# A hybrid layer on one core: the first dense weights in two transfers, h of tile 0 made by two engines, and finer waits for the first dense product

## The reference

```python
mod = silu(c) @ w_ada + b_ada            # six rows of 1024: sh1, sc1, gt1, sh2, sc2, gt2
h   = rms_norm(x, g_norm1) * (1 + sc1) + sh1
z   = h @ w_in + b_in                    # 1024 x 5376: u | v | q | k | v | gate A | gate B
ya  = gmlp_spatial(gelu(u), gelu(v))     # layer norm of v, 128 x 128 mixing by head
yb  = attention(rope(q), rope(k), v)     # windows of two chunks of 64, sinks
x   = x + gt1 * ((sigmoid(gA) * (ya @ w_o_a) + sigmoid(gB) * (yb @ w_o_b)) @ w_out)
h2  = rms_norm(x, g_norm2) * (1 + sc2) + sh2
x   = x + gt2 * moe(h2)                  # top 4 of 32 experts, 1024 x 2048 and 1024 x 1024 each
out = rms_norm(x, g_final)
```

## Time and profile before

| | us |
|---|---|
| median of 3 runs | 1270.43 (1270.15 to 1270.64) |
| the profiled execution | 1271.66 |
| its span, first to last instruction | 1269.9 |
| TensorE busy | 1041.1 (82%) |
| VectorE busy | 435.4 (34%) |
| ScalarE busy | 203.6 (16%) |
| mean granted TensorE clock | 0.913 |

### The profile page before, as it was taken

One profiled execution on the slowest core, in us unless ns is written; L12 is line 12 of the kernel. 1 busy time (PEld: TensorE's weight loads), 2 busy tenths in 40 slices (PEclk: granted clock), 3 DMA queues, 4 the chain that ended last, 5 costly groups with the idle time before them and its releaser, 6 DMA issues.

```text
span 1269.9 us, 26048 instructions
## 1 busy us (share of the span) xinstructions
PE 1041.1 (82%) x10163; PEld 507.8 (40%) x10164; DVE 435.4 (34%) x1050; ACT 203.6 (16%) x381; POOL 12.2 (1%) x39
## 2 busy tenths in 40 slices
PE   4799999977999678665999999999765679957774
PEld 1667777763444123221444444444222224422231
DVE  1885878875322113111222232233111113211122
ACT  2221223032121001000111112111100002100011
POOL 1100000000000000000000000000000000000000
PEclk9899999986999879877999999999878789987888
DMA  9987876697999999999969999939999997999996
GB/s 345 371 283 244 288 250 238 227 387 291 427 426 425 425 426 424 426 425 423 426 288 424 427 426 424 424 122 427 427 426 423 426 426 291 427 426 425 425 426 256
DMA packets 73035, 474.39 MB, mean 374 GB/s; under 512 B 7512, under 2 KB 9496, under 8 KB 39036
## 3 DMA queue, kind: packets, MB, share of 16 engines
q1 hardware_dynamic: 69888, 469.39, 90.2%
q10 hardware_dynamic: 2588, 3.03, 0.8%
q0 software_dynamic: 480, 0.83, 0.3%
HBM read 472.17 MB, written 1.06 MB: 373 GB/s over the span
## 4 chain that ended last, share of the span: by engine, by line
PE 50%; SPq 24%; DMA 19%; issue 3%; DVE 3%; ACT 1%; DVEq 0%; ACTq 0%
PE bank L1731 16%; DMA gate_up<-in_w_down_dram 14%; SPq L403 13%; PE acc L1364 13%; PE bank L1766 8%; SPq L391 8%; DMA down<-in_w_down_dram 3%; PE acc L1693 2%; PE bank L1675 2%; DMA gate_up<-in_w_in_dram 1%; DMA gate_up<-in_w_ada_dram 1%; PE bank L1681 1%; SPq L380 1%; SPq L515 1%; PE bank L1751 1%
## 5 line engine op out<-in xcount | busy, mean ns | idle before, releaser
L1731 PE MATMUL bank<-gate_up,mod 128*32 128x512 f32 x2512 | 337.4, 668 | 114.9 <-DMA gate_up<-in_w_gate_up_dram 94.9
L1731 PEld LDWEIGHTS bank<-gate_up,mod 128*32 128x32 f32 x2512 | 82.7, 117 | 305.6 <-issue 174.5
L1766 PE MATMUL bank<-gate_up,mod 128*32 128x256 f32 x2528 | 148.6, 381 | 11.3 <-DMA gate_up<-in_w_down_dram 9.9
L1364 PE MATMUL acc<-gate_up_r 128*128 128x512 f32 (+1 forms) x544 | 135.2, 395 | 7.5 <-DVE down_r L840 7.5
L787 ACT ACTIVATE front<-front 128x256 f32<-128x256 f32 x50 | 20.8, 416 | 727.2 <-DVE front L1298 727.2
L1298 DVE TENSOR_SCALAR front<-bank 128x256 f32<-128x256 f32 x50 | 21.2, 425 | 336.2 <-PE bank L1731 336.2
L1364 PEld LDWEIGHTS acc<-gate_up_r 128*128 128x128 f32 x544 | 100.6, 192 | 33.7 <-DVE down_r L840 8.0
L1766 PEld LDWEIGHTS bank<-gate_up,mod 128*32 128x32 f32 x2528 | 76.6, 110 | 70.7 <-DMA gate_up<-in_w_down_dram 17.3
L1314 DVE TENSOR_TENSOR mod<-bank,mod 128x256 f32<-128x256 f32 x50 | 21.2, 425 | 219.2 <-PE bank L1766 219.2
L1731 PE MATMUL bank<-down,mod 128*32 128x512 f32 x448 | 63.3, 690 | 27.0 <-DMA down<-in_w_gate_up_dram 24.8
L1218 DVE TENSOR_SCALAR front<-front 128x2 f32 x100 | 22.9, 229 | 154.1 <-issue 152.7
(11 more groups left out here) (309 smaller groups left out, 764.1 us busy)
## 6 DMA issues: line engine op xcount, KB each, us to landing
gate_up<-in_w_gate_up_dram SPq DMA_DIRECT2D x87, 2048.0 KB, 37.1
gate_up<-in_w_down_dram SPq DMA_DIRECT2D x96, 1024.0 KB, 34.5
down<-in_w_gate_up_dram SPq DMA_DIRECT2D x21, 2048.0 KB, 35.0
gate_up<-in_w_ada_dram SPq DMA_DIRECT2D x12, 2048.0 KB, 13.9
x_room<-in_w_gate_up_dram SPq DMA_DIRECT2D x12, 2048.0 KB, 34.1
down<-in_w_down_dram SPq DMA_DIRECT2D x22, 1024.0 KB, 35.4
gate_up<-in_w_in_dram SPq DMA_DIRECT2D x10, 2048.0 KB, 9.6
gate_up<-in_w_gate_up_dram SPq DMA_DIRECT2D x12, 1024.0 KB, 8.0
```

The lines of the kernel that those rows point to most:

```text
L1364: last = pe.matmul(bank[:, 0:cols], lhsT[:, k, rows], w[:, k, 0:cols], start=(n == 0 and k == 0), stop=(n == 2 and k == KC - 1))
L1731: last = pe.matmul(banks[4][q * BM:(q + 1) * BM, :], xT[:, k % KG, k // KG, :], w[:, :, q * HW:(q + 1) * HW], start=(k == 0), stop=(k == K ...
L1766: last = pe.matmul(banks[7][q * BM:(q + 1) * BM, 0:HW], hidT[:, k % KG, k // KG, :], in_groups(w[:, k % 2, :])[:, q], start=(k == 0), stop ...
```

## The change

The load of v0's weights is issued as two transfers, chunks 0 to 3 (counted by the new `v0_half_in`) and chunks 4 to 7 (`ring_in[0]`). VectorE casts the first half right behind the addition of b_ada, ahead of mod_col, and the second half after the cast of h of tile 0. The second half of h of tile 0 (bank xT01) is made by VectorE with four TENSOR_SCALAR, ScalarE makes the first half (xT00) and all of tile 1. VectorE counts the cast of h of tile 0 apart (`hT_upper`) from the subtraction (`hT_parts`), and subtracts for v0's weights in two halves (`w_lower_half`, `w_lower_dve`). TensorE's v0t0 waits for each of these where it first reads it, no longer for all of h's split at its start. Nothing else is moved, and what is computed stays the same.

```diff
@@ -295,6 +295,7 @@
         x_in, cond_in, gmlp_in, attn_in, route_in = (sem(n) for n in ("x_in", "cond_in", "gmlp_in", "attn_in", "route_in"))
         c_in, b_ada_in, ln_in, g2_in, gf_in, bd_in, stored = (sem(n) for n in ("c_in", "b_ada_in", "ln_in", "g2_in", "gf_in", "bd_in", "stored"))
         exp_bias_in = sem("exp_bias_in")
+        v0_half_in = sem("v0_half_in")
         mod_stored, gt1_in, sc2_in, sh2_in = (sem(n) for n in ("mod_stored", "gt1_in", "sc2_in", "sh2_in"))
         pair_in = [sem(f"pair_in{i}") for i in range(4)]
         ring_in = [sem(f"ring_in{i}") for i in range(RING + 1)]
@@ -450,7 +451,11 @@
                     cols = dense[i][2].shape[1]
                     sp.dma_start(bias_ring[:, i % 2, 0:cols],
                                  dense[i][2].to_broadcast([P, cols])).then_inc(bias_in[i % 2], 16)
-            load(*dense[0][:2], "ada1")
+            item_used(sp, "ada1")
+            for a in range(2):
+                chunks = slice(4 * a, 4 * a + 4)
+                sp.dma_start(ring[0][:, chunks, :], dense[0][1].rearrange("(k p) n -> p k n", p=P)[:, chunks, :])\
+                  .then_inc((v0_half_in, ring_in[0])[a], 16)
             load_bias(0)
             load(*dense[1][:2], "ada1")
             load_bias(1)
@@ -638,7 +643,7 @@
 
             act.wait_ge(ev("mod_col_ready"), 2)
             for t in range(TILES):
-                for h in range(2):
+                for h in range(1 if t == 0 else 2):
                     name = f"xT{t}{h}"
                     bank = z_wait(act, name)
                     for i in range(4):
@@ -884,18 +889,36 @@
             dve.wait_ge(ev("rows_made"), 4)
             dve.tensor_tensor(mod[:, 0:4, :].rearrange("p j n -> p (j n)"), mod[:, 0:4, :].rearrange("p j n -> p (j n)"),
                               banks[6][:, :], ALU.add).then_inc(ev("ada_added"), 1)
+            dve.wait_ge(v0_half_in, 16)
+            upper(w_upper[0][:, 0:4, :], ring[0][:, 0:4, :]).then_inc(ev("w_upper_half"), 1)
             dve.wait_ge(ev("modT_done"), 1)
             link(dve.tensor_copy(mod_col.rearrange("p s k -> p (s k)"),
                                  banks[5][:, :].rearrange("p (m n) -> p m n", n=QR)[:, :, 0]))
             dve.scalar_tensor_tensor(mul1, mod_col[:, 1, :], 1.0, g1_col, ALU.add, ALU.mult)\
                .then_inc(ev("mod_col_ready"), 2)
-            w_parts_upper(0)
-            for t in range(TILES):
-                for h in range(2):
-                    z_gone(dve, f"xT{t}{h}")
-                x_parts(hT, upper_a, hT_lower, "hT_parts", slice(t * P, (t + 1) * P))
-                if t == 0:
-                    w_parts_lower(0)
+            dve.wait_ge(ev("mod_col_ready"), 2)
+            bank = z_wait(dve, "xT01")
+            for i in range(4):
+                k = 4 + i
+                last = dve.tensor_scalar(hT[:, k, 0:P], bank[:, i * P:(i + 1) * P], mul1[:, k:k + 1], mod_col[:, 0, k:k + 1],
+                                         ALU.mult, ALU.add)
+            z_done(last, "xT01")
+            for h in range(2):
+                z_gone(dve, f"xT0{h}")
+            first_tile = slice(0, P)
+            upper(upper_a[:, :, first_tile], hT[:, :, first_tile]).then_inc(ev("hT_upper"), 1)
+            dve.wait_ge(ring_in[0], 16)
+            upper(w_upper[0][:, 4:8, :], ring[0][:, 4:8, :]).then_inc(ev("w_upper_ready"), 1)
+            dve.wait_ge(ev("hT_upper"), 1)
+            dve.tensor_tensor(hT_lower[:, :, first_tile], hT[:, :, first_tile], upper_a[:, :, first_tile], ALU.subtract)\
+               .then_inc(ev("hT_parts"), 1)
+            dve.wait_ge(ev("w_upper_half"), 1)
+            lower(dve, 0, slice(0, 4)).then_inc(ev("w_lower_half"), 1)
+            dve.wait_ge(ev("w_upper_ready"), 1)
+            lower(dve, 0, slice(4, 8)).then_inc(ev("w_lower_dve"), 1)
+            for h in range(2):
+                z_gone(dve, f"xT1{h}")
+            x_parts(hT, upper_a, hT_lower, "hT_parts", slice(P, 2 * P))
             w_parts_upper(1)
             w_parts_lower(1)
 
@@ -1356,11 +1379,24 @@
                 rows, low, up = slice(t * P, (t + 1) * P), *x
                 name = f"{item}t{t}"
                 bank = z_open(name)
-                pe.wait_ge(ev("w_upper_ready"), i + 1)
+                if name == "v0t0":
+                    pe.wait_ge(ev("hT_upper"), 1)
+                    pe.wait_ge(ev("w_upper_half"), 1)
+                else:
+                    pe.wait_ge(ev("w_upper_ready"), i + 1)
                 for n, (lhsT, w) in enumerate(((up, w_upper[i % 2]), (low, w_upper[i % 2]), (up, w_lower[i % RING]))):
+                    if n == 1 and name == "v0t0":
+                        pe.wait_ge(ev("hT_parts"), 1)
                     if n == 2:
-                        pe.wait_ge(ev("w_lower_dve"), i + 1)
+                        if name == "v0t0":
+                            pe.wait_ge(ev("w_lower_half"), 1)
+                        else:
+                            pe.wait_ge(ev("w_lower_dve"), i + 1)
                     for k in range(KC):
+                        if name == "v0t0" and k == 4 and n == 0:
+                            pe.wait_ge(ev("w_upper_ready"), 1)
+                        if name == "v0t0" and k == 4 and n == 2:
+                            pe.wait_ge(ev("w_lower_dve"), 1)
                         last = pe.matmul(bank[:, 0:cols], lhsT[:, k, rows], w[:, k, 0:cols],
                                          start=(n == 0 and k == 0), stop=(n == 2 and k == KC - 1))
                 z_put(last, name)
@@ -1439,7 +1475,6 @@
                 last = pe.transpose(banks[5][:, j * P:(j + 1) * P], mod[:, j, :], ident[:, :])
             last.then_inc(ev("modT_done"), 1)
             for n, item in enumerate(("v0", "v1", "u0", "u1")):
-                pe.wait_ge(ev("hT_parts"), 1)
                 rows_times(item, 0, h_parts)
                 pe.wait_ge(ev("hT_parts"), 2)
                 if n >= 2:
```

More of the change, by code:

```diff
@@ L52 @@
           "down_used", "ex_ready", "exp_done", "g_ready", "gates_ready", "gt_done", "gT_ready",
-          "gu_used", "h2_ready", "heads_ready", "hid_ready", "hidT_ready", "hot_ready", "ht_done", "hT_parts",
+          "gu_used", "h2_ready", "heads_ready", "hT_upper", "hid_ready", "hidT_ready", "hot_ready", "ht_done", "hT_parts",
           "mask_ready", "merged_ready", "mod_col_ready", "mod_zeroed", "modT_done", "mT_parts", "negm_ready", "negtop_ready",
@@ L57 @@
           "slot_gate_ready", "slots_ready", "ssq_ready", "std_ready", "table_ready", "trig_ready", "u_gelu",
-          "u_ready", "v_gelu", "var_ready", "vec_steps", "vn_ready", "vp_ready", "w_lower_dve",
+          "u_ready", "v_gelu", "var_ready", "vec_steps", "vn_ready", "vp_ready", "w_lower_dve", "w_lower_half", "w_upper_half",
           "w_upper_ready", "ws_masked", "x2_ready", "xe_ready", "xg_done", "xn_ready", "xt_done", "xT_ready",
```

## The result

| | us |
|---|---|
| before, median of 22 runs | 1272.10 (1269.77 to 1273.97) |
| changed, median of 22 runs | 1270.69 (1268.01 to 1273.64) |
| ratio | 0.9988, 95% interval 0.9983 to 0.9994 |
| changed, the profiled execution | 1273.64, span 1271.9 |

The kernel is faster by 1.5 us (0.12%; by the interval 0.8 to 2.2), where 2.4 were forecast (the medians differ by 1.4). Both kernels spread over more than 4 us between executions of the same program; the three runs shown before the prediction (1270.15 to 1270.64) were a narrow and low sample of it.

What follows compares the result with a forecast made beforehand. The prediction took TensorE for half the chain, SP's queue and DMA for most of the rest, with VectorE setting v0t1's start. 2.42 us off the median of 1270.43 gave 1268.0, range 1267.2 to 1270.0.

Steps and rivals of the forecast that it cites:

- 48.45 - 46.03 = 2.42: Start of product v0t1 on TensorE: from 48.45 to 46.03 us, a saving of 2.42 us.
- ada5 moves along: Transfer behind ada4: issued 2.42 us earlier to nearly idle DMA engines, it lands as much earlier, matmuls at 78.0.
- that rival: At ada5: it still lands at 80.38, the wait grows from 1.86 to 4.3 us, time 1270.4; chance 0.14.
- four signs of being wrong: VectorE waiting beyond 33.6, v0t0 ending after 46, ada5's wait above 1.9, no shift of 2.4 at 309 us.
- Steps 1 to 6 on VectorE: VectorE's order from the first half's cast (33.45) to tile 1's split (45.98); v0t0 starts at 37.44, v0t1 at 46.03.
- It waits for neither half: TensorE in v0t0's last third, reached at 43.4 to 44.3: no wait for either half of the weight subtraction.
- step 5: On VectorE: two halves of v0's weight subtraction, 2.29 us each, done at 41.90 and 44.11.
- 32.3 to 33.6: Time in us between which the first half of v0's weights would have landed; 33.4 was taken.
- the prediction's other reading, 33.6: First half's landing with a fixed 2.0 us per transfer: 33.6 us, the sum 0.15 less, 1268.2.
- Some 5 us after the start: TensorE's clock in v0t0: half clock for 5.0 us from its start, so v0t0 ends at 45.3.
- The sum for n: Slow matmuls among v0t0's 24 before the change, at 0.43 us against 0.227, 7.93 us in all: 11.3 to 11.7.
- v0t0 of before could be slow for longer: Rival on the clock before the change: 1.6 us longer slow gives a saving of 3.2, time 1267.2; chance 0.14.

Runs made afterwards that it cites:

- e9: The changed kernel with v0t1 started at the cast of h of tile 1, no longer its split; ratio to the kernel before 0.9977 (0.9968 to 0.9986).
- e8: The changed kernel with twelve unused matmuls of 128 columns on TensorE ahead of v0t0; ratio 0.9985 (0.9976 to 0.9994).
- e4: The changed kernel with the cast of the first half of v0's weights waiting for both halves; ratio 0.9996 (0.9987 to 1.0006).
- e13: The kernel before with seven unused matmuls behind the last modulation piece, to make the addition late; ratio 1.0004 (0.9995 to 1.0013).

## Why the prediction was right and wrong

**The measured time lies outside the range; the sign and the mechanism up to ada4 were right.** 1270.69 against 1267.2 to 1270.0.

- *The sum was taken off the median of three runs* (1270.43). With 22 runs it is 1272.10: 1.7 us of the 2.7 by which the forecast is off. The traces show the same: from the experts' first matmul to the end of the span it took between 960.7 and 964.2 us in 18 traces of identical code.
- *The term that was mis-sized is "48.45 - 46.03 = 2.42"*, the saving at the start of v0t1, carried unchanged to the end. In the first two traces it is 48.45 - 45.81, and at ada4 2.46, so as a reading of that trace it was right. Two things behind it were not. It holds for an early addition and a long v0t0 before; with a late addition, as in most traces, ada4 gains about 1.2 (0.7 and 1.3 in the two pairs of traces that share one). The step asked only what the new wait for v0's half costs, not what the old wait for v0 had hidden: under it a late addition cost 0.2 us at v0t0 (40.73 for 33.79), and costs all of its 1.0 now.
- *The step that failed in the early case is "ada5 moves along".* It landed 15.8 and 16.4 us behind ada4 in the two traces of the changed kernel with an early addition, against 15.5 before, so part of the gain was met by the transfer, as that rival had it, and the clock that fell at the end of the wait took 1.4 and 1.6 us more from the 16 matmuls alone. At ada6 0.0 to 0.4 us were left. With a late addition it landed 14.9 and 14.95 behind, and 1.4 to 1.9 us were there. In e9 it was 15.25, with ada4 at 62.52, nearly as early as in the first two; so an early ada4 isn't the whole reason, and what sets the landing is open. The time, 1.4 us by the medians, lies between the two cases; that it does so by their shares is an estimate from 13 traces.
- *Of the four signs of being wrong* two came: ada5's wait grew beyond 1.9 (2.16), and the shift at 309 us was not 2.4 but 0.9. VectorE did not wait for the half, and v0t0 ended at 45.14, before 46.
- *Steps 1 to 6 on VectorE* are right within 0.25 us: mul1's end 35.05 forecast and 34.96 seen, v0t0 37.44 and 37.32, the split of tile 1 45.98 and 45.75. So is that VectorE sets the start of v0t1 (e8), and that each us by which the cast of the first half starts later costs one (e4). "It waits for neither half" in step 5 was wrong by 0.23 us, since TensorE reached the last third at 42.65 and not at 43.4 to 44.3; VectorE's split hid it.
- *The first half* landed at 32.2, at the near bound of 32.3 to 33.6, and not at 33.4; the prediction's other reading, 33.6, is further off. The section that it takes the fixed 2.0 us from (the Trainium skill, "DMA: Bandwidth & Descriptors", "Anatomy of one DMA") describes transfers that GpSimd issues, and these are SP's. Neither changed the sum, as the half had 1.1 us to spare.
- *The clock.* "Some 5 us after the start" was a reading of one trace: by stretches of 1 us it came back 3.8 us after v0t0's start in the changed kernel (at 41.1), and 2.9 to 5.9 us after it in the other traces in which it had fallen. That VectorE hides it was right in all traces of the changed kernel. The sum for n doesn't come out as stated either: 24 matmuls in 7.93 us at 0.43 and 0.227 give 12.2 slow ones, not 11.3 to 11.7; it moved nothing. That v0t0 of before could be slow for longer and the saving larger went the other way: it is slow for shorter in all the other traces. And the clock at ada5's wait was nobody's rival: the 16 matmuls behind it were slow in the two traces with waits of 2.16 and 2.71 us, and in none of the ten with 1.19 to 1.93.
- *Behind 95 us* both kernels vary by more than the shift (211.65 to 213.58 us to the experts, 215.56 in e13); no run here tells a loss of the size of 0.5 us there from none.

Left open: why the addition is early or late in a given execution. The fourth piece lands at 29.3 to 29.8 us either way. In the early traces the third piece's matmuls are slow (3.2 to 3.4 us), the wait for the fourth is 1.6 to 1.8 us, and its matmuls take 1.92; in the late ones that wait is 2.0 to 3.1, and the fourth piece's matmuls are slow (2.8 to 3.6 us), which is the lateness. What decides between the two is not shown.

## What to carry to other kernels

A wait that a change removes may have hidden the lateness of something else. Ask what else ends in its shadow, and how much that varies, before its whole length goes into the sum. And follow the gain past the next transfer: here the executions that gained most at ada4 had least left at ada6. For a step of a tenth of a per cent take the time from many runs, and the size of the step as a distance between marks in several traces (here the addition of the modulation to ada4), since that distance repeated to 0.05 us in six of seven traces of the changed kernel while the ends of the same executions lay 4 us apart.
